# Order of the recurrence's norm, the Fourier products and the attention's first step in the mixers of a two-block transformer

## What is computed

```python
a_q, a_i, a_zf, a_zb, a_g, b_u, c_q, c_k, c_v = jnp.split(proj, SPLIT_POINTS, axis=-1)
o_a = hgrn2_mixer(a_q, a_i, a_zf, a_zb, a_g, lb_all[layer])
o_b = fourier_mixer(b_u)
o_c = dilated_attention_mixer(c_q, c_k, c_v, positions)
x = x + jnp.concatenate([o_a, o_b, o_c], axis=-1) @ w_out[layer]
```

## Time and profile before

| | us |
|---|---|
| Median of three runs | 2367.85 |
| Lowest, highest | 2366.20, 2368.78 |
| The profiled execution | 2370.25 |
| Its span | 2368.4 |
| TensorE matmuls busy | 2234.1 (94%) |
| VectorE busy | 1317.6 (56%) |
| ScalarE busy | 895.4 (38%) |
| GpSimd busy | 215.2 (9%) |

### The profile page before, as it was taken

How to read it: one execution, slowest core, us unless ns; L and a number is a source line. 1 busy time by engine, 2 the same in 40 slices (tenths; PEclk the granted TensorE clock), 3 DMA queues, 4 the chain that set the end, 5 groups by cost and what they waited for, 6 DMA issues and landing times.

```text
span 2368.4 us, 33737 instructions
## 1 busy us (share of the span) xinstructions
PE 2234.1 (94%) x14488; PEld 1721.5 (73%) x14488; DVE 1317.6 (56%) x1927; ACT 895.4 (38%) x1325; POOL 215.2 (9%) x170
## 2 busy tenths in 40 slices
PE   8998999999999988999999998998899998999994
PEld 6877478888888775688888876565788658677762
DVE  8655646425436574655335455565533264777775
ACT  6322643212233323642223332244221124666663
POOL 1122010000000121010000110000000001122221
PEclk9999999999999999999999999999999998999997
DMA  4111112232222112022222221211211325689884
GB/s 178 61 47 37 54 63 98 89 104 92 96 100 72 56 53 72 1 89 100 96 92 104 89 93 38 99 62 54 73 64 38 109 89 198 263 335 357 343 331 174
DMA packets 51992, 270.21 MB, mean 114 GB/s; under 512 B 12160, under 2 KB 12288, under 8 KB 22784
## 3 DMA queue, kind: packets, MB, share of 16 engines
q1 hardware_dynamic: 42048, 258.73, 29.9%
q0 software_dynamic: 9216, 8.42, 1.1%
q10 hardware_dynamic: 576, 0.87, 0.1%
HBM read 266.92 MB, written 26.21 MB: 124 GB/s over the span
## 4 chain that ended last, share of the span: by engine, by line
PE 84%; DVE 9%; ACT 4%; issue 1%; DMA 1%; SPq 0%; DVEq 0%; POOLq 0%; ACTq 0%
PE psum L123 81%; PE psum L126 3%; DVE A_mix L136 2%; DVE A_second L136 1%; ACT A_mix L130 1%; DVE A_mix L156 1%; DVE WL L136 1%; DVE A_second L144 1%; ACT WH L130 1%; ACT A_mix L133 1%; DMA M<-in_m 0%; DVE A_mix L162 0%; DVE A_mix L153 0%; ACT A_second L130 0%; DVE A_second L150 0%
## 5 line engine op out<-in xcount | busy, mean ns | idle before, releaser
L136 DVE TENSOR_TENSOR WL<-raw,WH 128x1024 fp32r<-128x1024 f32 x236 | 299.8, 1272 | 382.6 <-ACT WH L130 382.2
L130 ACT ACTIVATE WH<-raw 128x1024 fp32r<-128x1024 f32 x236 | 248.2, 1054 | 406.5 <-PE psum L123 394.6
L123 PE MATMUL psum<-HH,WH 128*128 128x512 f32 x736 | 306.1, 416 | 23.0 <-DVE A_second L136 11.5
L123 PE MATMUL psum<-R_op,WH 128*128 128x512 f32 x1024 | 316.2, 390 | 0.0
L123 PE MATMUL psum<-R_ffn,WH 128*128 128x512 f32 x1024 | 315.3, 389 | 0.0
L123 PE MATMUL psum<-HL,WH 128*128 128x512 f32 x736 | 293.6, 399 | 0.0
L123 PE MATMUL psum<-HH,WL 128*128 128x512 f32 x736 | 293.2, 398 | 0.0
L123 PEld LDWEIGHTS psum<-R_op,WH 128*128 128x128 f32 x1024 | 192.2, 188 | 40.8 <-issue 1.0
L123 PEld LDWEIGHTS psum<-R_ffn,WH 128*128 128x128 f32 x1024 | 192.2, 188 | 39.9
L123 PE MATMUL psum<-R_ffn,WL 128*128 128x512 f32 x512 | 199.2, 389 | 0.0
L123 PE MATMUL psum<-R_op,WL 128*128 128x512 f32 x512 | 199.2, 389 | 0.0
(11 more groups left out here) (199 smaller groups left out, 2934.5 us busy)
## 6 DMA issues: line engine op xcount, KB each, us to landing
ring_moe<-in_w_gu SPq DMA_DIRECT2D x64, 1024.0 KB, 10.0
raw<-in_w_in SPq DMA_DIRECT2D x41, 1024.0 KB, 4.8
raw<-in_w_up SPq DMA_DIRECT2D x32, 1024.0 KB, 4.8
raw<-in_w_down SPq DMA_DIRECT2D x32, 1024.0 KB, 4.8
ring_moe<-in_w_dn SPq DMA_DIRECT2D x32, 1024.0 KB, 7.1
raw<-in_w_out SPq DMA_DIRECT2D x12, 1024.0 KB, 4.8
kept<-A_second SPq DMA_DIRECT2D x20, 256.0 KB, 2.1
raw<-in_dft SPq DMA_DIRECT2D x4, 1024.0 KB, 4.8
```

Source lines behind the costliest of these rows:

```text
L123: return self.raw.matmul(o, l, r, start=start, stop=stop)
L130: return self.raw.activation(o, i, f, scale=scale)
L136: return self.raw.tensor_tensor(o, a, b, op)
```

## The change

The tail of the weaving string is changed from `cucuc` to `cuuucuc`. A new function `four_with` takes two steps of the Fourier part, then one of the attention, then the rest of both. TensorE's attention gets a `yield` behind the first scores where `free` is given, which is so in these two layers alone, and the first scores also wait until the copies of Fourier part 0 have left banks 0 and 1 (`fou_act`, 0, 1). The same is done for TensorE, ScalarE and VectorE; GpSimd has no step in the reordered stretch.

```diff
--- before.py
+++ after.py
@@ -1323,6 +1323,8 @@
                 t.then_inc(*did("att_pe", ly, "o", p))
 
             score(0)
+            if free:
+                yield
             for p in range(19):
                 if 2 <= p < 18:
                     turned(p - 2)
@@ -1382,6 +1384,16 @@
         def full(qt):
             return S
 
+        def four_with(four, att):
+
+            for _ in range(2):
+                next(four)
+                yield
+            next(att)
+            yield
+            yield from four
+            yield from att
+
         def win_pe(e, x):
             def total():
                 if x.ly == 0:
@@ -1394,6 +1406,7 @@
 
             def ready(e):
                 e.wait_ge(*at("rot_dve", x.ly, "a", 7))
+                e.wait_ge(*at("fou_act", x.ly, 0, 1))
 
             def free(e):
                 e.wait_ge(*at("fou_dve", x.ly, "lo", 3))
@@ -1401,8 +1414,8 @@
             yield from between(pe_lins(e, x.head + x.tail), **{f"s{0 if x.ly else 1}": total},
                                s3=lambda: pe_column(e, 2 * x.ly - 1),
                                **{f"s{ROT + i}": lambda i=i: rot_pe(e, x, i) for i in range(8)})
-            yield from four_pe(e, x)
-            yield from att_pe(e, x.ly, scores, lambda h, k: x.cv3[:, k, h * 64:(h + 1) * 64], x, full, ready, free=free)
+            att = att_pe(e, x.ly, scores, lambda h, k: x.cv3[:, k, h * 64:(h + 1) * 64], x, full, ready, free=free)
+            yield from four_with(four_pe(e, x), att)
 
         def first_square(e, i):
             if i in (3, 4, 5, 6, 7):
@@ -1425,8 +1438,7 @@
                 steps["s2"] = steps["s3"] = lambda: next(sines)
                 sines = act_tables(e, 64, x.tab, 64)
             yield from between(act_lins(e, x.head + x.tail, True), **steps)
-            yield from four_act(e, x)
-            yield from att_act(e, x.ly, x, full, evac)
+            yield from four_with(four_act(e, x), att_act(e, x.ly, x, full, evac))
 
         def win_dve(e, x):
             def evac(e, hp):
@@ -1449,13 +1461,12 @@
             for i in range(9):
                 steps[f"s{ROT + i}"] = lambda i=i: rot_dve(e, x, i)
             yield from between(dve_lins(e, x.head + x.tail, True), **steps)
-            yield from four_dve(e, x)
-            yield from att_dve(e, x.ly, x, full, mask, -0.125, evac)
+            yield from four_with(four_dve(e, x), att_dve(e, x.ly, x, full, mask, -0.125, evac))
 
         def win_pool(e, x):
             yield from between(range(48), **{f"s{ROT + i}": lambda i=i: rot_pool(e, x, i) for i in range(8)})
 
-        MIX = "u" * 14 + "cuucu" * 11 + "cucuc"
+        MIX = "u" * 14 + "cuucu" * 11 + "cuuucuc"
```

## The result

| | us |
|---|---|
| Before, median of seven runs | 2368.78 (2366.20 to 2371.72) |
| Changed, median of seven runs | 2376.25 (2372.08 to 2383.01) |
| Ratio changed to before, with its 95% interval | 1.0034 [1.0025, 1.0044] |
| The profiled execution of the changed kernel | 2372.08, its span 2370.3 |
| Predicted | 2375.4, from 2371.0 to 2380.5 |

The changed kernel is 0.34% slower by the ratio, 8 us with an interval of 6 to 10; the two medians lie 7.5 apart, and the forecast was 7.5.

A forecast was written before the change was run, and what follows sets the result against it. TensorE, busy 94% of the span, bounds the kernel through idle and lower clock. Idle 7.0 us plus clock 0.5 gives 7.5, applied to the unprofiled median 2367.85: 2375.4 us, range 2371.0 to 2380.5.

The forecast's parts named there:

- idle before part 0: TensorE between the last linear step and the first Fourier product: idle of 1.0 us in place of 2.32.
- wait for the reciprocal: TensorE out of work after scores 0, before the norm's expansion: 3.4 us idle until VectorE's reciprocal is done.
- wait of scores 2: TensorE before the attention's third score step, waiting for VectorE's row minima 1: some 2.2 us.
- half clock, before: Time at 1.2 instead of 2.4 GHz in the unchanged kernel: 3.74 us, all in the second layer's two stretches.
- Rival 5: No effect: streams drain so that the order on the engines stays what it was; 2367.9 us, chance 0.04.
- the squares' place on ScalarE: Norm's squares now queue behind the part 1 copies, leaving the norm's chain uncovered; the prediction called this what counts.
- rival 4: Norm hidden, faster: squares run before the part 1 copies, chain fits beneath part 1; 2362.0 us, chance 0.03.
- The idle term: TensorE's added idle from the last linear step to scores 2: 3.5 us a layer, 7.0 in two.
- The clock term: Half clock after idles: 2.1 us a layer, 4.2 in all against 3.74 before, +0.5 net, from -3.7 to +3.8.
- the first idle: TensorE's idle of 3.4 us before the expansion and the closing pair, taken to cost 1.3 us of clock a layer.
- the second idle: TensorE's idle of 2.2 us before scores 2, either-way kind: 40% of 2, so 0.8 us of clock a layer.
- The table load: ScalarE's load between squares and root: 1.28 us without a drain; with the drain 1.4 longer a layer, near 2378.2.

The follow-up runs named there:

- filled kernel: Three needless matmuls filling TensorE's idle before the wait for the reciprocal, against the changed kernel; 2373.27 us against 2369.14 before, ratio 1.0010.
- The first repair: Against the changed kernel: squares ahead of ScalarE's row copies, sum, root and reciprocal between Fourier parts 0 and 1; 2369.61 us against 2370.47 before, ratio 0.9999.
- the best version: Against the kernel before: ScalarE's row copies ahead of the norm's root, attention's first step ahead of the closing pair; 2355.08 against 2370.47, again 2355.02 against 2369.79 us.

## Why the prediction was right

By its steps, in us of one layer:

| step | predicted | measured |
|---|---|---|
| idle before part 0 | 1.0 | 1.02 |
| parts 0 and 1 back to back | 14.1 | 13.97 |
| wait for the first square | 1.5 | 1.57 |
| the sum, unpaired | 1.6 | 1.56 |
| wait for the reciprocal | 3.4 | 3.27 |
| wait of scores 1 | none | none |
| wait of scores 2 | 2.2 | 2.01 (filled kernel), 1.57 (changed) |
| loss in idle time | 3.5 | 3.05 |
| half clock, changed | 2.1 | 2.6 |
| half clock, before | 1.87 | 2.06 |
| two layers, in all | 7.5 | 7.3 |

**The mechanism** is shown, not only argued, for the move of the norm as a whole: with the reciprocal out of the chain the loss disappears, with the norm alone moved it is there in full, and with the early step alone it is a gain. Rival 5 falls by the timelines.

**What the prediction says too much** is that the squares' place on ScalarE is what counts, and by rival 4 what decides. The sum stands behind part 1 on TensorE, which is in order, so root and reciprocal could not run beneath part 1 even with the squares done. An estimate from rows: with early squares the expansion would start 1.10 (sum to root), 0.71 (root to reciprocal) and 3.40 (reciprocal to expansion) behind part 1's end, 5.2 instead of the measured 7.5, and of its wait some 3.1 of 3.27 would stay, the sum and scores 0 covering 2.1. So the squares' queue is worth about 2.3 a layer and the place of the norm's sum the rest; no run moved the squares alone. The first repair hid the root and the reciprocal because it moved the sum ahead of part 1 as well, and it did not reach rival 4's 2362.0: that rival also left out VectorE's work behind the expansion.

**The idle term** was 0.45 a layer too large. Counted from the group of 56, the prediction puts the expansion at 30.8, scores 1 at 35.4 and scores 2 at 38.7; in the filled kernel they start at 30.5, 35.2 and 38.3. So most of the error stands ahead of the expansion: 0.13 is a slip (233.07, 7.03 and 6.97 make 247.07, not 247.2), and the two squares took 1.15 together where the prediction has 1.25. What is left are hundredths in rows that had not stood back to back before.

**The clock term** was 0.5 a layer too small in the changed kernel, for the half clock takes the whole closing pair, where I had reckoned with 1.3 for the first idle and 0.8 for the second. In the changed kernel the second idle never brought a fall of its own; the first one brought a longer one. The 40% that the prediction took for it was a guess. The two errors cancel in the sum, by luck, so the forecast of 7.5 against the 7.5 between the medians is closer than its terms deserve; that 2375.4 stands 0.85 under 2376.25 is the first median of before, 0.9 under that of seven runs.

**The table load.** By the rule of the Trainium skill ("ScalarE: Activation LUTs", "What ACT_TABLE_LOAD costs") a drain of about 1.38 would have stood beside the load of 1.28. Here the squares end at 244.40, the load runs from 244.41 to 245.69, the root starts at 245.70 and the sum that it needs had ended at 245.49: nothing is there but the load. By that rule the expansion's wait would have been about 4.65 (an estimate, 3.27 and the page's 1.38); it was 3.27. Leaving the drain out was right for this kernel.

## What to carry to other kernels

When a chain that crosses engines is moved behind other work, write down for every link what stands before it in its own engine's queue, and then what it pushes back there: here the sum fell behind both products and the squares behind copies that wait for the second, and in the repair the expansion's products fell in front of the row minima. A wait before the main engine may be the order of two short operations on a side engine; exchanging these two was worth about as much as the whole rearrangement lost. In this kernel the idle of 3.27 us on TensorE cost 2.6 more in clock behind it, four times out of four, nearly its own length again; the idle of 2.32 cost 1.7 more in the second layer (8.80 against 7.11) and nothing in the first. Look at more than one execution before such a price goes into a sum.

## What the runs showed of the hardware beyond what I expected

- Half clock that falls on work with a parallel chain costs less than its length: the expansion and the closing pair were 2.7 longer (7.4 against 4.7), the tail 2.4, mostly because the wait for row minima 1 shrank from 2.01 to 1.57.
- The same idle can bring the lower clock in one place of a program and not in another: behind 2.32 us of it the second layer's part 0 fell in three executions of three, the first layer's in none. The waits of 1.57 and 1.40 at the scores were followed by a fall in four of the six layers that have both and no longer wait ahead of them (two executions of before, one of the root moved alone).
- The tail without a fall repeats to 0.01 us (36.72 in two executions of two layers each), while whole executions of one kernel in one comparison lie up to 15 us apart (before, 2362.92 to 2377.60). The scatter goes with the granted clock: the kernel before had 0.976 and 0.970 in these two, the changed kernel took 2372.08 at a mean clock of 0.975 and 2383.01 at 0.969, the best version 2352.49 at 0.979 and 2356.63 at 0.976. What decides in an execution where it falls was not tried.
